# A two-layer hybrid transformer on one core: the decay bias of the forgetting attention by way of memory instead of through TensorE

## The reference, cut to what matters

```
logf = log_sigmoid(zf + b_f)                    # zf: (256, 16), from the same projection as v
c = cumsum(logf over tokens)                    # per head
logit[t, s] = q_t . k_s / sqrt(64) + c_t - c_s  # s <= t, else -1e30
out = softmax(logit) @ v
```

## Time and profile before

| | |
|---|---|
| median of 3 runs | 1610.99 us (1610.56 to 1611.12) |
| span of the profiled execution, first to last instruction | 1607.8 us |
| its own time beside the span | not given for this kernel; the median lies 3.2 us above the span |
| PE busy | 1592.8 us, 99% |
| DVE, ACT, POOL busy | 1092.2, 920.2 and 53.9 us |
| DMA | 287.67 MB, 179 GB/s in the mean |
| fox phase, from its first projection to the end of its output projection | about 1299 to 1415 us |

### The profile page before, as it was taken

How to read it: one execution, slowest core, us unless ns; L and a number is a source line. 1 busy time by engine, 2 the same in 40 slices (tenths; PEclk the granted TensorE clock), 3 DMA queues, 4 the chain that set the end, 5 groups by cost and what they waited for, 6 DMA issues and landing times.

```text
span 1607.8 us, 23572 instructions
## 1 busy us (share of the span) xinstructions
PE 1592.8 (99%) x9247; PEld 1356.0 (84%) x9247; DVE 1092.2 (68%) x1759; ACT 920.2 (57%) x1553; POOL 53.9 (3%) x96
## 2 busy tenths in 40 slices
PE   8999999999999999999999999999999999999998
PEld 6887888889888888888887788888888889888887
DVE  5877776778667777665677566567666667775665
ACT  5756754567665555644576564456454474674544
POOL 4000000000030000000002100000000000000000
PEclk9999999999999999999999999999999999999999
DMA  8444666546355555656555465654665654456562
GB/s 293 136 145 153 232 224 192 188 145 197 94 196 187 192 175 177 212 175 203 185 153 182 118 208 183 196 185 158 221 185 185 193 189 148 124 173 204 187 185 77
DMA packets 212225, 287.67 MB, mean 179 GB/s; under 512 B 11052, under 2 KB 180334, under 8 KB 212116
## 3 DMA queue, kind: packets, MB, share of 16 engines
q1 hardware_dynamic: 208500, 280.00, 55.0%
q0 software_dynamic: 3616, 6.17, 1.4%
HBM read 284.47 MB, written 3.87 MB: 179 GB/s over the span
## 4 chain that ended last, share of the span: by engine, by line
PE 96%; DMA 1%; DVE 1%; ACT 1%; SPq 0%; issue 0%; POOL 0%; DVEq 0%
PE two L2191 89%; PE two L2268 1%; PE two L2450 1%; PE two L2437 1%; PE two L2460 1%; DMA x_tok<-in_x 1%; DVE w_lo L1462 1%; PE two L2575 0%; PE two L2823 0%; PE two L2254 0%; DMA vals<-u_dram 0%; PE two L2463 0%; ACT p_sb L1033 0%; DMA u_dram<-aux 0%; PE two L2431 0%
## 5 line engine op out<-in xcount | busy, mean ns | idle before, releaser
L2191 PE MATMUL two<-act_parts,w_hi 128*128 128x512 f32 (+1 forms) x2784 | 802.0, 353 | 0.0
L1462 DVE TENSOR_TENSOR w_lo<-raw,w_hi 128x1024 fp32r<-128x1024 f32 (+1 forms) x520 | 612.9, 1220 | 114.8 <-ACT w_hi L844 114.3
L2191 PE MATMUL two<-act_parts,w_lo 128*128 128x256 f32 x2256 | 634.9, 281 | 0.0
L2191 PEld LDWEIGHTS two<-act_parts,w_hi 128*128 128x128 f32 x2784 | 486.9, 188 | 82.0 <-issue 6.2
L844 ACT CAST w_hi<-raw 128x1024 fp32r<-128x1024 f32 (+1 forms) x520 | 516.3, 1048 | 6.1 <-DMA raw<-in_ffn_w_up 4.5
L2191 PEld LDWEIGHTS two<-act_parts,w_lo 128*128 128x128 f32 x2256 | 425.5, 189 | 2.1
L2191 PE MATMUL two<-w_hi,act_parts 128*128 128x512 f32 (+2 forms) x832 | 249.8, 380 | 2.4 <-ACT w_hi L844 2.3
L973 ACT COPY p_sb<-two 128x512 f32<-128x512 f32 x108 | 62.5, 579 | 247.0 <-PE two L2191 247.0
L2191 PE MATMUL two<-w_hi,hid_even 128*128 128x512 f32 x576 | 187.8, 393 | 0.0
L2191 PEld LDWEIGHTS two<-w_hi,act_parts 128*128 128x128 f32 x832 | 151.5, 189 | 33.4 <-issue 3.0
L1590 DVE TENSOR_TENSOR pt_sb<-two,p_sb 128x512 f32<-128x512 f32 x54 | 37.3, 691 | 198.5 <-ACT p_sb L973 198.5
(11 more groups left out here) (317 smaller groups left out, 1199.5 us busy)
## 6 DMA issues: line engine op xcount, KB each, us to landing
raw<-in_ffn_w_up SPq DMA_DIRECT2D x160, 512.0 KB, 4.0
raw<-in_ffn_w_down SPq DMA_DIRECT2D x132, 512.0 KB, 3.5
raw<-in_ffn_w_gate SPq DMA_DIRECT2D x80, 512.0 KB, 3.8
raw<-in_a_w_in SPq DMA_DIRECT2D x24, 512.0 KB, 4.6
raw<-in_fox_w_in SPq DMA_DIRECT2D x20, 512.0 KB, 3.7
raw<-in_ffn_w_up SPq DMA_DIRECT2D x32, 256.0 KB, 3.6
raw<-in_w_kv SPq DMA_DIRECT2D x12, 512.0 KB, 3.6
raw<-in_mem_w_kv SPq DMA_DIRECT2D x8, 512.0 KB, 10.7
```

Source lines behind the costliest of these rows:

```text
L1462: nc.vector.tensor_tensor(w_lo[:, r, 0:n], raw[:, r, 0:n], w_hi[:, r, 0:n], ALU.subtract).then_inc(lo_done, 1)
L2191: return nc.tensor.matmul(dst, a, w, start=start, stop=stop, skip_group_check=True)
```

## The change

PE's `f_turn` and L2431 are gone, and with them `f_sums`, `pick`, `rowf` and the wait for `gates_m` on PE. `cumulate_rows` makes the sums as rows at once: the log gates are the weights (16 columns), the triangle moves (256 and 128 columns). It stands before `fox_part(0, 0, 0)`, two quarters of a projection earlier. DVE's `f_rows` is one instruction, which scales and negates 16 rows, and it stands before `splits(433)`; the separate `splits(432)` is dropped, so that slot 432 is made behind it. POOL writes the rows to `decay_dram` with two DMAs, waits for both, and for each pair reads two rows back, spread over all 128 partitions (128 x 768 numbers, 384 KB), into one of four buffers, issues the next read, and adds the causal mask with one two-input instruction. DVE's `scores` waits for this (`bias_ready`) and takes the result where it took `causal`. A buffer is read into again once the maxima of four pairs before are done. The last gain row stands behind all of this, with the wait it had.

```diff
+        fox_bias = [misc[:, 0:2 * CAUSAL], misc[:, 2 * CAUSAL:4 * CAUSAL], aux[:, 3840:3840 + 2 * CAUSAL],
+                    mk[:, :, :, :].rearrange("p a c t -> p (a c t)")[:, 0:2 * CAUSAL]]
...
-            for p, row in ((2, norm_g_2[0, 5]), (3, norm_g_2[1, 1]), (4, norm_g_2[1, 3]), (5, norm_g_2[1, 5])):
+            for p, row in ((2, norm_g_2[0, 5]), (3, norm_g_2[1, 1]), (4, norm_g_2[1, 3])):
                 pool.wait_ge(hg_done, 4 * p)
                 gain_row(row)
+            def read_decays(n):
+                if n >= 4:
+                    pool.wait_ge(h_max, PAIR0["fox"] + n - 3)
+                pool.dma_start(fox_bias[n % 4],
+                               bass.AP(tensor=decay_dram.tensor, offset=2 * n * CAUSAL, ap=[[0, P], [1, 2 * CAUSAL]])).then_inc(decay_in, 16)
+            def mask_decays(n):
+                rows = fox_bias[n % 4].rearrange("p (a k) -> p a k", a=2)
+                nc.gpsimd.tensor_tensor(rows, rows, causal[:, :].rearrange("p (a k) -> p a k", a=1).to_broadcast([P, 2, CAUSAL]),
+                                        ALU.add).then_inc(bias_ready, 1)
+            pool.wait_ge(gates_m, 2)
+            pool.dma_start(decay_dram[:, 0:P], rowc[0:FOX_H, 0:P]).then_inc(decay_out, 16)
+            pool.dma_start(decay_dram[:, P:CAUSAL], rowc[0:FOX_H, :]).then_inc(decay_out, 16)
+            pool.wait_ge(decay_out, 32)
+            read_decays(0)
+            for n in range(FOX_H // 2):
+                pool.wait_ge(decay_in, 16 * (n + 1))
+                if n + 1 < FOX_H // 2:
+                    read_decays(n + 1)
+                mask_decays(n)
+            pool.wait_ge(hg_done, 20)
+            gain_row(norm_g_2[1, 5])
...
+                    elif kind == "fox":
+                        dve.wait_ge(bias_ready, n + 1)
...
-                        bias = swab[:, n % 2, half * CAUSAL:(half + 1) * CAUSAL] if kind == "swa" else causal[:, :]
+                        bias = (swab[:, n % 2, :] if kind == "swa" else fox_bias[n % 4])[:, half * CAUSAL:(half + 1) * CAUSAL]
...
-            def f_sums():
-                dve.wait_ge(gates_c, 2)
-                step(nc.vector.memset(c_wide[:, :, :], 0.0))
...
-                dve.wait_ge(gates_t, 2)
...
+            def f_rows():
+                dve.wait_ge(gates_c, 2)
+                nc.vector.tensor_scalar(rowc[0:FOX_H, :], st[0:FOX_H, SEQ:2 * SEQ], -DH ** 0.5, None, ALU.mult).then_inc(gates_m, 1)
...
-                        nc.tensor.matmul(dst[half][:, 0:CAUSAL], pick[rows, h0 + half:h0 + half + 1].to_broadcast([DH, P]), rowf[rows, :],
-                                         start=True, stop=False, skip_group_check=True)
...
+            def cumulate_rows(k):
+                pe.wait_ge(gates_lf, 2)
+                nc.tensor.matmul(st[0:k, SEQ:2 * SEQ], lf_sb[:, 0, 0:k], tri[:, :], start=True, stop=False, skip_group_check=True)
+                nc.tensor.matmul(st[0:k, SEQ + P:2 * SEQ], lf_sb[:, 1, 0:k], tri[:, 0:P], start=False, stop=True,
+                                 skip_group_check=True).then_inc(gates_c, 1)
...
             project("FVA", 1)
+            cumulate_rows(FOX_H)
             fox_part(0, 0, 0)
-            cumulate(2, FOX_H)
             fox_part(0, 0, 1)
-            f_turn()
             fox_part(0, 1, 0)
             fox_part(0, 1, 1)
-            pe.wait_ge(gates_m, 2)
```

More of the change, by code:

```diff
@@ L293, in build @@
         rs = sb("rs", [P, NTB])
-        with nc.sbuf_tensor("rowf", [P, CAUSAL], F32R) as rowf:
-            pass
         misc = sb("misc", [P, 4 * CAUSAL])
@@ L301, in build @@
         tab_dram = nc.dram_tensor("tab_dram", [B_HEADS, 512], F32, kind="Internal").ap()
+        decay_dram = nc.dram_tensor("decay_dram", [FOX_H, CAUSAL], F32, kind="Internal").ap()
         tab_rows = nc.dram_tensor("tab_rows", [B_HEADS, P * CAUSAL], F32, kind="Internal").ap()
@@ L524, in build @@
         kswap_in = sem("kswap_in")
+        decay_out = sem("decay_out")
+        decay_in = sem("decay_in")
+        bias_ready = sem("bias_ready")
         cw_ps = sem("cw_ps")
@@ L2154, in _ @@
             sigmoid_end(2, FOX_H, 0)
-            splits(432)
-            f_sums()
+            f_rows()
             splits(433)
-            f_rows()
             take_pair(0, 0)
@@ L2427, in scores @@
                 dst = [place[g][:, half * 512:(half + 1) * 512] for half in range(2)]
-                for half in range(2):
-                    if kind == "fox":
-                        rows = slice(DH * half, DH * half + DH)
-                        nc.tensor.matmul(dst[half][:, 0:CAUSAL], pick[rows, h0 + half:h0 + half + 1].to_broadcast([DH, P]), rowf[rows, :],
-                                         start=True, stop=False, skip_group_check=True)
                 for b, (lo, hi) in enumerate(cuts(kind)):
@@ L2437, in scores @@
                         ins = nc.tensor.matmul(dst[half][:, lo:hi], q[:, b * P:(b + 1) * P], k[:, 0:hi - lo],
-                                               start=kind != "fox", stop=True, skip_group_check=True)
+                                               start=True, stop=True, skip_group_check=True)
                 ins.then_inc(h_s, 1)
@@ L2478, in attention, with cumulate @@
                         between(n)
-            def cumulate(n, k):
-                pe.wait_ge(gates_lf, n)
+            def cumulate(k):
+                pe.wait_ge(gates_lf, 1)
                 nc.tensor.matmul(st[:, 64:64 + k], tri[:, 0:P], lf_sb[:, 0, 0:k], start=True, stop=True)
@@ L2620, in _ @@
             project("VO0", 1)
-            cumulate(1, A_HEADS)
+            cumulate(A_HEADS)
             for b in range(NTB):
@@ L2903, in _ @@
             ffn(4, False)
[L2906 to L2910, removed]
             def fox_part(m, which, i):
```

1 line of the change is left out of this document (removed).

## The result

The changed kernel takes 1612.56 us, median of 18 runs (1610.87 to 1616.04), against 1610.59 us for the kernel before, median of 18 (1609.17 to 1612.49). The ratio is 1.0016, with a 95% interval of 1.0010 to 1.0022: about 2 us slower (1.97 by the medians; by the means of all runs, 1613.14 and 1610.65, it is 2.5). That is inside the predicted range and under 0.2%, but on the other side of the forecast, which was 0.9 us faster. The profiled execution took 1611.83 us, its span is 1610.1 us: 2.3 us above the span before. In every execution whose span is given beside its time, the time lies 1.7 or 1.8 us above that span. The 3.2 us read before the change was the distance of one execution's span to the median of others, and no constant: by 1607.8 + 1.7 the profiled execution before took about 1609.5 us (an estimate), 1.1 us less than its kernel's median.

The account below looks back on a forecast made before the run. PE's own stream was taken to bound the fox phase. Shortening it by 1.2 + 0.2 - 0.3 = 1.1 us, less 0.2 us of stall, gave -0.9 us: 1610.1 us, range 1607.8 to 1613.0.

Parts of the forecast that it names:

- Term 1: PE's bias matmuls (L2431) about the fox scores: removing them saves 0.15 us per pair, 1.2 us for eight pairs.
- Rival 1: PE at the fox scores: the whole slot of L2431 is saved, 2.96 us, giving 1608.1 us; chance 0.10.
- Terms 2 and 3: PE's gate sums: dropping f_turn's two transposes saves 0.2 us, cumulate_rows costs 0.3 us more than cumulate; they nearly cancel.
- Term 2: PE's f_turn: two transposes go, taken as 0.2 us saved.
- Rival 4: Odd pairs: PE's stream is shorter, but loops between DVE and ACT take it back, 1611.0 us; chance 0.12.
- The bias in time: POOL's way to pair 0's scores: first mask ready about 1336.4, nominally 3.7 us early, at worst 0.4 late; no stall.
- Rival 3: POOL's bias chain is late for the scores and PE stalls one for one: 1626 us; chance 0.06.
- DVE against POOL: SBUF work of both engines meeting in the fox phase: about 0.5 us per meeting, 0.2 us of stall at pair 3.
- Rival 2: POOL's masks hold DVE for their whole length before turns: 1616.1 us, half of meetings 1613; chance 0.12, half or whole.
- The cushion of pair 0: Between the end of DVE's probs of pair 0 and PE's turn: 2.07 us of room.

Follow-up runs that it names:

- e5: Kernel before without its sixteen bias matmuls (L2431), nothing else changed: 1608.95 us against 1610.20, ratio 0.9991.
- e1: Changed kernel without POOL's eight masking instructions, DVE's scores waiting for the landed read instead: 1609.19 us against 1610.29 for the kernel before, ratio 0.9992.
- e6: Kernel before with eight idle masking additions on POOL in unused memory, each started just in front of its pair's divisions: 1616.45 us against 1610.20, ratio 1.0037.
- e2: Changed kernel with masks from pair 2 on held back until the divisions of the odd pair in front are done: 1609.47 us, ratio 0.9994 to the kernel before.
- e4: Changed kernel with each mask made by two GpSimd selections of 256 columns instead of one addition of 768: 1609.28 us, ratio 0.9996 to the kernel before.
- e8: Changed kernel with selection masks, first four reads issued at once, later masks waiting for divisions of pairs 1 and 3: 1609.05 us against 1610.20 for the kernel before.
- e10: Same kernel as e8, counted again beside the changed kernel on the same chip: 1609.12 us against 1610.57 for the kernel before, ratio 0.9990.
- e3: Changed kernel with the fox division written as a product of two SBUF inputs: 1613.20 us, ratio 1.0019 to the kernel before.
- e7: Changed kernel with each mask added twice, one behind the other on POOL: 1628.25 us against 1610.20 for the kernel before, ratio 1.0109.
- e9: Changed kernel again with no edit, on the chip of e10: 1612.51 us against 1610.57 for the kernel before, ratio 1.0013.

## Why the prediction was wrong in its sign and right in its sum for PE

**Term 1, right.** 1.07 us about the scores against 1.08 predicted, and the 64-row matmul begins 0.21 behind the projection as predicted. e5 has the term alone at 1.25 us against 1.2. By the timelines it is a little more, 8 x 0.17 = 1.4 us. Rival 1 falls.

**Terms 2 and 3, right together.** From the first matmul of the sums to the next projection 0.85 us was predicted and 0.75 measured; 0.85 it is only with the 0.1 us at the entry. So the sums cost 0.27 us more than before, against 0.3 in the sum. Term 2 was not measured by itself. e1, which has all three terms and no mask, is at -1.1 us, the number of the sum. Rival 4 falls with it: in e1 no turn waits for a division, those of the odd pairs neither.

**The bias in time, right.** The first mask ended at 1335.02 + 1.84 = 1336.86, in a span that runs some 0.6 us later there; 1336.4 was predicted. The reads landed in 3.8, 4.5 and 5.2 us (lowest, median, highest), a mask took 1.84 for the estimated 1.86, POOL's round, from one read's issue to the next, was 4.1 to 5.5 us while it ran ahead (5 at most was predicted), and L1701 never waited for POOL. Rival 3 falls.

**DVE against POOL: the step that failed.** "So a meeting costs DVE about 0.5 us", and from it "I put 0.2 us of stall in the sum (0 to 0.5)". The runs show up to 1.93 us for one meeting (2217 ns for a division of 284), 3.0 us of waits on the weight loader and 2.4 on PE. Two things went wrong in that step.

The first is the row. The earlier trace rows is no meeting with a mask. The GpSimd instructions beside it are one-input ones (L799), and these did not hold a division to their end:

```profile
859.42 1.29 POOL L799 TENSOR_SCALAR misc<-dist 128x384 f32<-128x384 f32 x1
...
859.57 0.59 DVE L1696 TENSOR_SCALAR p_sb<-p_sb,small 128x256 f32<-128x256 f32 x1
```

This division began 0.15 us behind the GpSimd instruction and ended at 860.16, 0.55 us before it; the one behind it took its usual 0.27 us inside the same GpSimd instruction. The group of four lost 0.25 and 0.23 us at its two divisions of 256 columns. The GpSimd instruction of 2.23 us that the prediction counts to the same meeting is the next one; it began at 860.79, beside a `w_lo` subtraction from 860.78. A mask, an addition of two inputs, costs a division all that is left of it: 0.89 of the 1.08 us left at pair 1, 0.62 of the 0.82 left at pair 3, and its whole length at pair 0. Whether it is the two inputs that make the difference, no run shows.

The second is the room. It was set against one meeting at a time, and so only pair 3, with 0.2 us, was to stall. But delays carry over on DVE from an even pair to the odd one behind it: half of pair 1's 1.84 us came from pair 0, and e6 shows the same.

Rival 2 is the mechanism, a hold for the mask's whole length, and it had been given 0.12. Its "half of the meetings give 1613" fits the time, -1.1 + 3.0 = +1.9 us against +1.97 measured, but partly by luck: the 3.0 us stand on the weight loader and 2.4 on PE, and the rival has 1.7 us at pair 3 and 0.75 at the other late pairs, where the trace has 0.67 at pair 3, 1.84 at pair 1 and 0.51 at pair 0. e1 (no masks), e2 (masks elsewhere in time) and e6 (masks in the kernel before) each move the loss as this mechanism says; in e4, e8 and e10 no mask meets a division, and there is no loss.

Here the rule of the Trainium skill, "SBUF — State Buffer" (the shared port pair, held as an exclusive lock for a whole instruction, two-input DVE instructions included), was set aside for a figure that looked milder. For the masks the runs agree with it: e3's two-input form took 2281 ns. For L799 the trace before does not: the division above was not held to the end of the GpSimd instruction.

**Only the first pairs stall.** The rival put a room of 1.1 us at each late pair and asked for all of them. In the trace the meetings fell on pairs 0, 1 and 3; the eighth and last mask ends at 1371.42 + 2.00 = 1373.42, and the divisions of pair 4 begin only at 1381.81 (1.01 us, undisturbed). So the masks run out before half of the turns have come. The cushion of pair 0, 2.07 us in the prediction, was also smaller than read: without the hold its divisions would have ended at 1344.94 + 1.01 = 1345.95 and PE would have turned at 1347.94 - 0.51 = 1347.43, a room of 1.48 us. The group took 2.94 - 1.01 = 1.93 us too long, 0.45 more than that room, and PE stood for 0.51.

**What stays open.** 3.0 us on the weight loader are 2.4 us on PE in the waits, and the windows agree (1.94 + 0.46 = 2.40). The profiled span lies 2.3 us above before, where -1.1 + 2.4 would be 1.3. The 1 us between is within what single executions of either kernel differ by, and was not followed further. Nor is it shown what a short or a one-input GpSimd instruction would do to a division in this phase: e4 changed both at once, and its selections met none.

## What to carry to other kernels

Price GpSimd work that runs beside DVE by the length of its single instructions, not by its sum. A two-input addition of 1.84 us held a DVE instruction for all of that here. What counts is whether the room in front of the next turn of PE is longer than all that DVE has lost since the last turn that had to wait, and not the loss of that pair alone. If it isn't, move the work to where DVE has no division (e2, e8), or write it as something shorter (an addition of 1.84 us as two selections of 0.39 brought 1.97 + 1.01 = 3.0 us here, in a run in which no selection met a division). And when an old row is taken as the price of a conflict, look first at whether the same two forms of instruction meet in it, and how they overlap.

## What was not expected of the hardware

The holding works in both directions. The mask at 1340.50, which began while DVE's last `w_lo` subtraction in front of the scores still ran (to 1341.08), took 2.28 us and not 1.84. The 2.23 us in the earlier trace rows were such a case too.

A stall of PE can cost more than itself. In e7 the granted clock fell to 0.66 in three windows of 5 us, each right behind a window in which PE had stood still, for 2.24, 3.57 and 4.46 us. In the profiled execution of e9 PE stood still for 1.69 and 1.47 us in two neighbouring windows of 5 us, and the clock was 1.00 in both and behind them. A fall may still lie behind the changed kernel's long runs: of its 18, the six between 1614.45 and 1616.04 us have a mean granted clock of 0.997 or 0.998, the twelve between 1610.87 and 1613.85 have 0.999 or 1.000; in e8 and e10, where no turn waits, no run is under 0.999. That is an association over whole executions, not a cause shown.
